# Softmax attention layer: order of turns, scores and values between two projections

## The reference, cut to what matters

```python
def branch_a(h, w_in, sinks, w_out, rel_bias):
    z = h @ w_in
    q, k, v, gate = jnp.split(
        z, [A_WIDTH, A_WIDTH + A_KV_WIDTH, A_WIDTH + 2 * A_KV_WIDTH], axis=-1)
    o = sliding_window_sink_attention(q, k, v, sinks, rel_bias).astype(h.dtype)
    return (o * jax.nn.silu(gate)) @ w_out

# in the attention, for each head:
    p = jax.nn.softmax(jnp.concatenate([s_meta, s_loc, sink], axis=-1), axis=-1)
    o = (jnp.einsum('bnhgqs,bshd->bnqhgd', p[..., :N_META], vm)
         + jnp.einsum('bnhgqs,bnshd->bnqhgd', p[..., N_META:N_META + 2 * BLOCK], vl))
```

## Time and profile before

| | |
|---|---|
| median of three runs | 905.19 us (904.98 to 906.22) |
| the profiled execution, its own time | 904.98 us |
| its span, first to last instruction | 903.1 us |
| TensorE matmuls busy | 894.1 us (99%) |
| VectorE busy | 556.5 us (62%) |
| ScalarE busy | 428.2 us (47%) |
| GpSimd busy | 62.8 us (7%) |

### The profile page before, as it was taken

One profiled execution on the slowest core, in us unless ns is written; L12 is line 12 of the kernel. 1 busy time (PEld: TensorE's weight loads), 2 busy tenths in 40 slices (PEclk: granted clock), 3 DMA queues, 4 the chain that ended last, 5 costly groups with the idle time before them and its releaser, 6 DMA issues.

```text
span 903.1 us, 17875 instructions
## 1 busy us (share of the span) xinstructions
PE 894.1 (99%) x7182; PEld 862.2 (95%) x7182; DVE 556.5 (62%) x744; ACT 428.2 (47%) x683; POOL 62.8 (7%) x85
## 2 busy tenths in 40 slices
PE   9999999999999999999999999999999999999997
PEld 9999999999999999899999999999999999988886
DVE  6578667667765767785646464555646355545546
ACT  6556455645655344375454343535444444435421
POOL 1322133113100000000000000000000000000000
PEclk9999999999999999999999999999999999999999
DMA  9774465455442555515453444444354534454622
GB/s 350 234 234 163 157 213 146 145 168 177 152 150 110 187 187 187 187 63 213 145 187 139 176 149 165 160 144 181 139 186 139 186 141 167 157 215 159 233 93 94
DMA packets 25256, 153.05 MB, mean 169 GB/s; under 512 B 3411, under 2 KB 3939, under 8 KB 8709
## 3 DMA queue, kind: packets, MB, share of 16 engines
q1 hardware_dynamic: 21600, 142.19, 43.9%
q0 software_dynamic: 2896, 7.70, 4.2%
q10 hardware_dynamic: 724, 2.66, 0.8%
HBM read 150.36 MB, written 2.18 MB: 169 GB/s over the span
## 4 chain that ended last, share of the span: by engine, by line
PE 94%; DMA 2%; DVE 2%; ACT 1%; SPq 1%; issue 0%; DVEq 0%
PE bank L333 70%; PE bank L703 10%; PE bank L448 2%; PE bank L488 2%; DMA work<-chunks 1%; DMA raw<-chunks 1%; PE bank L648 1%; PE bank L647 1%; PE bank L650 1%; PE bank L615 1%; PE bank L574 1%; PE bank L588 1%; DVE w_lo L1061 1%; PE bank L463 0%; PE bank L616 0%
## 5 line engine op out<-in xcount | busy, mean ns | idle before, releaser
L333 PE MATMUL bank<-x_hi,w_hi 128*128 128x272 f32 (+1 forms) x1472 | 425.6, 289 | 0.0
L333 PE MATMUL bank<-x_hi,w_lo 128*128 128x272 f32 (+1 forms) x1472 | 421.4, 286 | 0.0
L333 PE MATMUL bank<-x_lo,w_hi 128*128 128x272 f32 (+1 forms) x1472 | 421.3, 286 | 0.0
L1061 DVE TENSOR_TENSOR w_lo<-raw,w_hi 128x2048 fp32r<-128x2048 f32 x126 | 290.8, 2312 | 207.5 <-ACT w_hi L782 174.3
L782 ACT ACTIVATE w_hi<-raw 128x2048 fp32r<-128x2048 f32 x114 | 217.8, 1912 | 156.7 <-PE bank L333 108.2
L333 PEld LDWEIGHTS bank<-x_hi,w_hi 128*128 128x128 f32 x1472 | 277.4, 188 | 1.3 <-issue 0.4
L333 PEld LDWEIGHTS bank<-x_hi,w_lo 128*128 128x128 f32 x1472 | 277.3, 188 | 0.0
L333 PEld LDWEIGHTS bank<-x_lo,w_hi 128*128 128x128 f32 x1472 | 277.1, 188 | 0.0
L333 PE MATMUL bank<-og_hi,w_hi 128*128 128x272 f32 x240 | 70.1, 292 | 0.0
L333 PE MATMUL bank<-og_hi,w_lo 128*128 128x272 f32 x240 | 69.4, 289 | 0.0
L333 PE MATMUL bank<-og_lo,w_hi 128*128 128x272 f32 x240 | 69.1, 288 | 0.0
(11 more groups left out here) (243 smaller groups left out, 1019.0 us busy)
## 6 DMA issues: line engine op xcount, KB each, us to landing
raw<-chunks SPq DMA_DIRECT2D x128, 1024.0 KB, 4.8
work<-bias_table POOLq DMA_DIRECT2D x8, 512.0 KB, 5.6
work<-chunks SPq DMA_DIRECT2D x4, 512.0 KB, 12.4
work<-bias_table POOLq DMA_DIRECT2D x8, 256.0 KB, 6.6
work<-ln_rows ACTq DMA_DIRECT2D x1, 2048.0 KB, 7.3
out<-work SPq DMA_DIRECT2D x8, 256.0 KB, 2.4
h<-xT SPq DMA_DIRECT2D x2, 544.0 KB, 9.5
raw<-chunks SPq DMA_DIRECT2D x4, 256.0 KB, 5.1
```

Source lines behind the costliest of these rows:

```text
L333: last = mm(o, l, r, start=(kt == 0 and n == 0), stop=(kt == KT - 1 and n == 2))
L1061: V.tensor_tensor(lo_part, raw[:, half, :, :], hi_part.bitcast(f32), ALU.subtract) \
```

## The change

On TensorE the values of pair 1 of pass i - 1 leave the middle of the second projection of pass i and go to the middle of the first projection of pass i + 1, ahead of the turn there; the last pass does its own as before as well. The turn of pair 1 goes from between the two scores to ahead of both. ScalarE and VectorE do what belongs to those values (high part, gate, remainder) at the matching place of the next pass. GpSimd stages keys and bias of pass i first and then the values of pass i - 1, so that the value copies no longer stand ahead of the next key.

```diff
@@ -496,12 +496,18 @@
 
             def body_a(i, last):
                 Pg = P_Q0 + 2 * i
-                project(Pg, x_hi, x_lo, ALL, between=lambda: turn_a(i - 1, 0))
+
+                def values_and_turn():
+                    if not (isinstance(i, int) and i == 1):
+                        value_a(i - 2, 1)
+                    turn_a(i - 1, 0)
+
+                project(Pg, x_hi, x_lo, ALL, between=values_and_turn)
                 value_a(i - 1, 0)
-                scores_of(i, 0)
                 turn_a(i - 1, 1)
-                scores_of(i, 1)
-                project(Pg + 1, x_hi, x_lo, ALL, between=lambda: value_a(i - 1, 1))
+                for u in range(2):
+                    scores_of(i, u)
+                project(Pg + 1, x_hi, x_lo, ALL, between=(lambda: value_a(i - 1, 1)) if last else None)
 
             body_a(1, False)
             with pe.Fori(2, A_ITERS - 1) as i:
@@ -892,6 +898,7 @@
                 else:
                     split_hi(Pg + 2, 0)
                     copies(i - 1, 0)
+                    gated_hi(i - 2, 1)
                 gate_tanh(Pg, i - 1)
                 gated_hi(i - 1, 0)
                 split_hi(Pg + 2, 1)
@@ -899,8 +906,8 @@
                 exps(i)
                 if not last:
                     split_hi(Pg + 3, 0)
-                gated_hi(i - 1, 1)
                 if last:
+                    gated_hi(i - 1, 1)
                     gate_tanh(Pg + 1, i)
                     split_hi(Pg + 3, 0)
                 else:
@@ -1179,20 +1186,21 @@
             def body_a(i, last):
                 Pg = P_Q0 + 2 * i
                 split_lo(Pg + 2, 0)
+                if not (isinstance(i, int) and i == 1):
+                    gated(Pg - 2, i - 2, 1)
+                    gated_lo(i - 2, 1)
                 gates(Pg, i - 1)
                 gated(Pg, i - 1, 0)
                 row_maxima(i)
                 gated_lo(i - 1, 0)
                 split_lo(Pg + 2, 1)
-                gated(Pg, i - 1, 1)
+                if last:
+                    gated(Pg, i - 1, 1)
                 normalise(i)
                 if last:
                     gated_lo(i - 1, 1)
                     gates(Pg + 1, i)
-                    split_lo(Pg + 3, 0)
-                else:
-                    split_lo(Pg + 3, 0)
-                    gated_lo(i - 1, 1)
+                split_lo(Pg + 3, 0)
                 split_lo(Pg + 3, 1)
                 if not last:
                     queries_lo(i + 1)
@@ -1485,7 +1493,7 @@
             pool.wait_ge(tab_ready, 2)
             pool.dma_start(bass.AP(table, 0, [[TAB, 32], [1, TAB]]), setup["tab"][0:32, :]).then_inc(tab_stored, 16)
             pool.wait_ge(tab_stored, 16)
-            def stage(i, first):
+            def stage_keys(i, first):
 
                 ax = i // 4
                 if first:
@@ -1511,6 +1519,10 @@
                 hankel(bt[0:16, :, 416:432], 240, 16, 16)
                 pool.tensor_tensor(k_lo_cur, a["kT"][:, ax, :], k_hi_cur.bitcast(f32), ALU.subtract) \
                     .then_inc(k_staged, 1)
+
+            def stage_values(i, first):
+
+                ax = i // 4
                 if first:
                     pool.wait_ge(banks_cleared, 3)
                     pool.wait_ge(v_copied, 4)
@@ -1521,9 +1533,13 @@
                 pool.tensor_copy(a["V_cur"], V4[:, :, ax, :]).then_inc(v_staged, 1)
                 pool.tensor_copy(a["VL_cur"][0:16, :], VL4[0:16, ax, :]).then_inc(v_staged, 1)
 
-            stage(0, True)
-            with pool.Fori(1, A_ITERS) as i:
-                stage(i, False)
+            stage_keys(0, True)
+            stage_values(0, True)
+            stage_keys(1, False)
+            with pool.Fori(2, A_ITERS) as i:
+                stage_keys(i, False)
+                stage_values(i - 1, False)
+            stage_values(A_ITERS - 1, False)
 
 
 def backwards(ap):
```

## The result

The changed kernel takes 910.4 us in the median of six runs (910.0 to 910.59), the kernel before 905.35 in six (904.98 to 906.22). The ratio is 1.0055, with a 95% interval of 1.0044 to 1.0066: slower by 0.5%, 5.05 us. The forecast was 910.4 us in a range of 909.4 to 911.8.

The account below looks back on a forecast made before the run. TensorE's instruction order and waits were taken to bound the kernel; -0.3 us (values' move) and +5.6 us (turn's move) gave +5.2 on rounding, on a median of 905.19: 910.4 us, range 909.4 to 911.8.

Parts of the forecast that it names:

- The 911.2 given for the upper bound: Upper end of the span that the forecast with its bounds was said to cover, 909.4 to 911.2 us.
- Values out of the second projection: TensorE, passes 2 to 7: the first turn follows values, not a projection, 1.20 us against 1.25; -0.3 us in all.
- the price of the breaks: TensorE's step from projection to values costs 0.21 us extra, paid as often as before; projection to turn costs none.
- The lower bound of the step: Values' move, per pass: -0.26 us if the removed break gave back its whole 0.21 and the new one cost nothing.
- Second turn ahead: Second scores wait uncovered for VectorE's read of head 0's bank: 0.82 us in passes 2 to 6, +5.6 us in all.
- The choice of the full wait: Second scores: weight loads not pulled ahead over the semaphore wait; otherwise the sum is some 0.1 us per pass smaller.
- The accumulator's slack: Second projection's end: ScalarE empties the first accumulator at about 179.9, TensorE needs it at 180.9; slack 1.0 us, cost 0.
- The gate's: Slack of the moved gate ahead of the first pair's values, tightest in pass 6: 0.7 us, cost 0.
- The normalisation: VectorE, no longer sharing its time with GpSimd's bias DMAs: 2.54 us instead of 3.62, 1.1 us faster, off the path.
- (a): Rival: a second wait, from maxima stretched by DMA issues or a late moved gate; 911.5 to 913 us; 1 in 10.
- (b): Rival: the new wait is covered or the change doesn't reach TensorE's order as read; 904.9 us; 4 in 100.
- (c): Rival: faster, the second projection's middle break goes with its 0.21 us; 1.8 us gained, about 903.3; 3 in 100.

Follow-up runs that it names:

- the one run with the long wait: The changed kernel with the second scores waiting for the reads of two heads, not one: 921.88 us, ratio 1.0186 to the kernel before.
- the run with the turn between: The changed kernel with the second turn put back between the two scores, the values left in their new place: 904.69 us, ratio 0.9997 to the kernel before.
- the run with the turn first: Changed kernel, head 3 in bank 7, turn ahead of the values in the middle of the first projection (902.9 us), behind it (902.84) or both (901.89).

## Why the prediction was right

*The number.* That the median is the forecast to the tenth is luck. The forecast added 5.2 us to 905.19; the kernel before took 905.35 beside this run, and the medians moved by 5.05. The profiled execution took 910.53 us where 910.2 was forecast for it. The 911.2 given for the upper bound doesn't follow from the working: a gain of 0 and a wait of 6.4 us on 905.2 are 911.6. The range went beyond both.

*What bounds the kernel.* TensorE's order and waits, and in the one run with the long wait its clock, explained every run: no other engine's work changed the time, though VectorE's busy time fell by 6.6 us (556.5 to 549.9).

*Values out of the second projection: -0.3 us.* Right in its parts, too large as a sum. The turn behind values cost 1.20; the price of the breaks was unchanged. A small term was missing: the run of three halves took 18.35 us where 3 x 6.04 + 0.21 = 18.33, and the half behind such a turn 6.25, not 6.24. Together some 0.2 us over the layer, so that 0.1 us was gained and not 0.3 (0.16 by the run with the turn between). That is too small for the medians to tell. The lower bound of the step (the removed break gives all of its 0.21 back, the new one costs nothing) did not hold, but the run with the turn first shows that another order gets the 0.21 back.

*Second turn ahead: +5.6 us.* Right, by its own working: start to start 1.75 us in passes 2 to 6 as forecast, 1.85 in pass 7, and in pass 1 the scores start 76.51 - 73.46 = 3.05 us behind the values' end, against 2.45, so +0.60 where +0.56 was forecast. From the layer's first values to its last the changed kernel is 218.74 us long against 213.24: +5.5, where the sum gave +5.2. Waits of 5 x 0.82 + 0.92 + 0.60 = 5.6 less the 0.1 above make up these 5.5. The choice of the full wait was right: the weight loads stood still in it too (0.85 us in the row of pass 4). What the Trainium skill's page "TensorE: Matmul & The Clock Gate" says of loads pulled ahead (section "Architectural detail: the array is 16× 32×32, not 1× 128×128") did not reach over a semaphore wait in any pass.

*The slacks.* The accumulator's slack came out as worked, 1.0 us. The gate's was 2.9 us in pass 6, not 0.7: the forecast took the start of the weight split ahead of it from before, and that split starts 224.78, 5.5 us ahead of the values, where it had been 3.5. The normalisation, 1.1 us faster, frees the raw buffer sooner and can account for that much; no run shows it, and the rest stays open. Nor was pass 6 the tightest. In pass 7 the split starts 4.1 us ahead of the values, where it had been 5.1 (257.03 - 251.92), and the gate ends at 259.95 + 0.43 = 260.38, 1.5 us ahead of the values:

```profile
257.74 2.29 DVE L1068 TENSOR_TENSOR w_lo<-raw,w_hi 128x2048 fp32r<-128x2048 f32 x1 [4.18 <-ACT w_hi L788]
259.95 0.43 DVE L1166 SCALAR_TENSOR_TENSOR work<-bank,work 128x272 f32<-128x272 f32 x1
...
261.85 0.90 PEld L488 LDWEIGHTS bank<-work 128*64 128x64 f32 x12
```

The cost of 0 held, but neither slack was where the trace of the kernel before had it.

*The rivals.* (a), a second wait, didn't come: the maxima took 2.06 us with GpSimd's queue in its new place, as in the earlier trace rows. (b), the wait covered, is what the run with the turn between is, and there the forecast of 904.9 fits its 904.7. (c), faster, needed the wait gone; with the wait gone (head 3 in bank 7) its size was 1.3 us of the 1.8, mostly by way of the longer run of scores (0.6) and of the wait that pass 1 had already (0.4), and not of the break that it named.

## What to carry to other kernels

Ahead of moving an operation, ask what runs under it: a step that costs its own time wherever it stands can still be the cover of a read that somebody behind it waits for, and here 0.82 us of cover a pass was all that the change moved. A buffer that a change leaves free can be worth more than the change, as here: head 3's scores fit into the bank that the moved values no longer held (903.89 us), and with it the turns could be moved (901.89). Where TensorE is the bound, each step from one kind of operation to another is worth a look in the loads' starts (0.21 us from a projection to values here), and another operation between the two, here the turn, can take it away.

## What was not expected

A wait of 1.4 us on TensorE cost 2.9 us where the clock fell behind it (1.4 + 1.5), and a wait of 0.82 us cost itself. With one more head's read to wait for, the changed kernel lost 16.7 us on the kernel before, not 5. Ten useless matmuls in the wait made the kernel 7.3 us faster (921.88 to 914.56).

The scores of both pairs of heads in one run took 1.76 us, 0.09 less than apart.
